# Two-layer transformer block with modulation: the modulation products in half chunks and full chunks, one bias added on TensorE

## Chip, cores, metric

One core of one Trainium2 chip runs the whole program. The metric is the device time of one execution in microseconds, as the median of several runs.

## What is computed

The program computes a first block of two layers on 256 tokens of width 1024, all in float32, and a second block on its result. Only the parts that the change touches are shown; the first layer's attention and the modulation of the second block are:

```python
# first block, layer 0: differential attention, 8 heads, 256 tokens in 2 blocks of 128 queries
sc = einsum('bqhcd,bkhcd->bhcqk', q_blk, k) * scale      # c: two score maps per head, d = 64
sc = where(causal_mask, sc + bias, NEG_INF)              # bias: T5 table by distance and head
a = softmax(sc); wts = a[:, :, 0] - lam * a[:, :, 1]
o = einsum('bhqk,bkhv->bqhv', wts, v)
mix = rms_norm(o, sub_gain) * (1 - lam_init) @ w_o
h = h + mix
h = h + conv_gated_ffn(rms_norm(h, g), w_in, conv_w, conv_b, w_out)   # width 2816, gate, conv of 3 tokens
h = h + per_layer_embedding(...)                                       # then layer 1 (latent attention), the same
# second block, for i in 0, 1: c and c_ctx are two vectors of 1024, w_mod[i] is 1024 x 3072
mod_x = silu(c) @ w_mod[i] + b_mod[i]
mod_c = silu(c_ctx) @ w_mod[i] + b_mod[i]
sh, sc, g = split(mod, 3)
hx = rms_norm(x) * (1 + sc_x) + sh_x ; ... ; x = x + g_x * yx
```

The modulation of both layers depends on nothing of the first block. It is a product of two vectors with 1024 x 6144 weights, 24 MB of float32.

## The kernel before

Every engine has an order of work written out by hand, with semaphores between them. SP loads 295 weight panels of 512 KB in turn into a ring of six (`RAW`); ACT writes the high part of each (`WH`, L1848), DVE the low part (`WL`, L1131), and PE multiplies high by high, low by high and high by low (L417 to L419) in `gemm_unit` and its kin. These are fp32r products. Plain float32 products, transposes among them, are two records each in the trace.

**Modulation.** The 24 MB are 48 panels of 128 x 1024 (512 KB), loaded by POOL's DMAs into the tile `M`. Two stages use them while PE does other work.

- The first 16 panels (`PLAIN`) are used in the first attention, `l0`. Panel `i` holds 128 output columns, with 8 groups of 128 rows. `fill(n)` (L548, called L765 to L773) issues `n` products of `SC[:, k, :]` (silu of the vectors, 128 x 32) with a 128-column tile of the panel (L558), 32 rows by 128 columns of output, float32, into the bank `O` (in the trace, `R`). There are 128 such products: 12 ahead of the attention, 5 in each of its steps up to the 18th, 14 after it, and 6 behind each of two groups of transposes. POOL loads panels in `panels` (L2494, DMA L2499), a few ahead of each `head_squares` (L2523). The squares wait for a head's output (`at_g`).
- The other 32 panels are used in the two feed-forwards, one after each of 16 tiles of a feed-forward. POOL loads them in `gathers` (L2501); ACT writes a high part (`high`, L2081), DVE a low part (`rest`, L1524), and `refill` (L571) issues four fp32r products 32 x 512 (L578) with `SCR`, the vectors in high and low part. ACT copies each finished row out (`row`, L2086 and L2139). In the embedding part (`ple`) 16 transposes of 32 x 32 (`turn_gathered`, L587) bring them to columns, and DVE sums and adds `b_mod` (`gathered`, L1420).

**Attention `l0`.** `attention` on PE (L625) takes 16 units, for each head a unit of one tile of keys (`qt` = 0) and one of two (`qt` = 1). In step n PE does the scores of unit n (`scores_l0`, L742: two maps in two row groups of 64), the filler, the value products of unit n-3 if that ended a head (`value_l0`, L750), and the transposes of unit n-2 (L651), which subtract the two maps. DVE adds the bias to the scores (`bias_l0`, L1359, 128 x 256 or 128 x 512), takes the maximum (L1212) and scales (L1187 to L1193). ACT copies the transposed weights of unit n-2 (L1887), takes the exponentials of unit n (L1898), and copies a head's output (L1997). After it come the norm over heads (POOL L2523, DVE L1364, ACT L2007, DVE L1371 and L1375), eight transposes at a time (`heads_turn`, L759), their high and low parts (ACT L2013, DVE L1384), and the projection `l0_o`.

Of the kernel before, what the change touches and what calls it, by code (L numbers as in the profile page):

```python
# [23 lines left out]
P = 128  # L24
# [5 lines left out]
PT = 8  # L30
# [7 lines left out]
MODS = 48  # L38
PLAIN = 16
GROUPS = 4  # L40
# [95 lines left out]
def program(nc, x_tok, wst, wmod, vec, cst, x_t, ctx_t, p_t, pos, pos4, tab, rpb, lam4, grow, y_t):  # L136
    with ExitStack() as ctx:
# [31 lines left out]
        SCR = sb("SCR", [P, KD, 32], F32R)  # L169
# [51 lines left out]
        RM = mv[:, 6144:12288].rearrange("p (s c) -> p s c", s=RMS)  # L221
# [43 lines left out]
        YR = B[0:32, 2048:4608]  # L265
        RR = RM[:, 0:4, :]
        RH = XH[:, 12:16, :].rearrange("p n t -> p (n t)")
        RL = XL[:, 12:16, :].rearrange("p n t -> p (n t)")
        ROWS = HRS[:, 1, 0:32].rearrange("p (r t) -> p r t", r=2)
# [61 lines left out]
        r_raw = [sem(f"r_raw{i}") for i in range(4)]  # L331
        r_hi, r_lo, r_y = sem("r_hi"), sem("r_lo"), sem("r_y")
# [76 lines left out]
        def _(pe):  # L409
# [137 lines left out]

            def fill(n):  # L548

                for _ in range(n):  # L550
                    i, k = divmod(fills[0], KD)
                    if fills[0] == 0:
# [4 lines left out]
                    out = O  # L557
                    m = mm(out[32 * g:32 * g + 32, q * P:(q + 1) * P], SC[:, k, :], RM[:, i % RMS, k * P:(k + 1) * P],  # L558
                           start=(k == 0), stop=(k == KD - 1), skip_group_check=True)
                    if k == KD - 1:  # L560
                        m.then_inc(m_used, 1)
                    fills[0] += 1

            def turn_modulators(dst):

                pe.wait_ge(m_y, 1)
                for q in range(4):
                    m = nc.tensor.transpose(dst[:, q * P:(q + 1) * P], YS[:, q * P:(q + 1) * P], IDT)
                m.then_inc(m_tr, 1)

            def refill(layer, s, i):  # L571

                if s == 0:
                    pe.wait_ge(r_y, i + (2 + 5 * layer))
                pe.wait_ge(r_lo, i * 4 + (5 + PLAIN * layer + s))
                for c in range(2):
                    for w in (RH, RL):
                        m = mm(O[0:32, :], SCR[:, 2 * s + c, :], w[:, 512 * c:512 * c + 512],  # L578
                               start=(s == 0 and c == 0 and w is RH), stop=(s == 3 and c == 1 and w is RL),
                               skip_group_check=True)  # L580
                m.then_inc(m_used, 1)

            def turn_gathered(layer):

                pe.wait_ge(r_y, 1 + 5 * (layer + 1))
                for t in range(PLAIN):
                    m = nc.tensor.transpose(O[:, 32 * t:32 * t + 32], YR[:, 512 + t * P:512 + (t + 1) * P], IDT[0:32, 0:32])  # L587
                m.then_inc(m_tr, 1)
# [36 lines left out]
            def attention(s, scores, value, filler=0, behind=None, meanwhile=(0, 0), first=0, last=None, ready=()):  # L625
                units = attn_units(s)
                width = 1 if s == "l0" else 2
                for n in range(first, len(units) + 3 if last is None else last):
# [7 lines left out]
                    if n < len(units) + 2:  # L636
                        fill(filler)
# [138 lines left out]
            turn_modulators(A[0])  # L776

            def ffn(layer):
# [37 lines left out]
                def tile(j, i=0, filled=None):  # L816
# [4 lines left out]
                    if filled is not None:  # L821
                        refill(layer, filled, i)

                if layer == 0:
                    pe.wait_ge(m_ok, 1)
                for j in range(2, 7):
# [4 lines left out]
                for d in range(3):  # L831
                    tile(19 + d)
                    refill(layer, d, 3)
                down(0, p0 + 64, hb + FT - 1, p0 + 64, False, False)
                refill(layer, 3, 3)
                down(1, p0 + 65, hb + FT, p0 + 65, False, True)

            def ple(layer):
# [7 lines left out]
                for u in range(4):  # L846
# [4 lines left out]
                    if u == 0:  # L851
                        row_parts(b, False)
                        turn_gathered(layer)
# [56 lines left out]
            attention("l1", scores_l1, value_l1, 0, first_o, (4, 3), first=2, ready=((1, TVALS),))  # L910
# [115 lines left out]
            attention("a", scores_a, value_a, 0, first_o, (2, 2), first=4)  # L1026
# [73 lines left out]
            attention("b", scores_b, value_b, 0, first_o, (6, 3), first=2, ready=((0, TVALS + 10), (1, TVALS + 12)))  # L1100
# [17 lines left out]
        def _(dv):  # L1118
# [237 lines left out]
            def bias_l0(sc, un):  # L1356
                h, qt, nk, *_ = un
                k0 = 0 if qt == 0 else P
                return v.tensor_tensor(sc, sc, bc(TB[:, h, k0:k0 + nk * P], 2), ALU.add)  # L1359
# [37 lines left out]
            def with_bias(layer, r, t0, rows):  # L1397

                n = rows.shape[-1] if len(rows.shape) == 2 else rows.shape[-1] * rows.shape[-2]
                at = VC[f"bm{layer}"] + t0  # L1400
                dst, bias = MD[:, layer, r, t0:t0 + n], V[:, at:at + n]
                if len(rows.shape) == 3:
                    dst, bias = (x.rearrange("p (g q) -> p g q", q=4) for x in (dst, bias))
# [7 lines left out]
            def modulators():  # L1411

                dv.wait_ge(m_tr, 1)
                rows = A[0].rearrange("p (q g r) -> p r g q", q=4, g=4)
                for r in range(2):
                    with_bias(0, r, 0, rows[:, r, :, :])
                scales(0)
                v.memset(SM[:, 35:36], 0.0).then_inc(m_ok, 1)

            def gathered(e, parts):  # L1420

                dv.wait_ge(m_tr, e + 1)
                link(v.tensor_reduce(ROWS, O.rearrange("p (t x) -> p t x", x=32)[:, :, 0:4].rearrange("p t (s r) -> p r t s", s=2),
                                     AX, ALU.add))
                for layer, t0, a, b in parts:
                    for r in range(2):
                        with_bias(layer, r, t0, ROWS[:, r, a:b])
                if e == 2:
                    scales(1)
                v.memset(SM[:, 35 + e:36 + e], 0.0).then_inc(m_ok, 1)  # L1430
# [20 lines left out]
            modulators()  # L1451
            dv.wait_ge(m_sil, 1)
            link(v.tensor_copy(SCR[:, :, :], SC[:, :, :]))
            link(v.tensor_tensor(SCR[:, :, 2:4], SC[:, :, 0:2], SCR[:, :, 0:2].bitcast(F32), ALU.subtract))
            v.memset(SM[:, 34:35], 0.0).then_inc(r_y, 1)
            v.memset(SM[:, 39:40], 0.0).then_inc(r_lo, 4)
# [20 lines left out]
            def ffn(layer):  # L1477
# [43 lines left out]
                def rest(s, i):  # L1521

# [1213 lines left out]
```

## Time and profile before

| | |
|---|---|
| median of 3 runs | 1325.74 us |
| lowest, highest | 1325.57, 1326.34 us |
| profiled execution, span from first to last instruction | 1325.0 us (its own time is not listed apart from the span) |
| mean granted TensorE clock | 0.998 |
| busy: PE, DVE, ACT, POOL | 1271.4, 945.7, 723.9, 391.0 us |
| attention `l0` with its end | about 98.8 to 149.3 us of the span |
| feed-forward of layer 0, of layer 1: most of each | 155 to 390, 640 to 805 us |

Matmul records overlap, so their lengths add up to more than the time they take; the time from one start to the next is what PE pays. The chain of waits gives its pieces that way. A view by lines gives busy time, the mean length of one record, and the idle time before it with what ended it.

### The profile page before, as it was taken

The numbers are of one execution on the slowest core, as the hardware profiler recorded it, in microseconds if no ns is written. First come the engines' busy times: TensorE is split into PE (matmuls) and PEld (weight loads), VectorE is DVE, ScalarE is ACT, GpSimd is POOL, SyncE is SP. The second block draws the span as 40 slices with busy tenths as digits, with TensorE's granted clock in tenths as the row PEclk, the third lists the DMA queues.
The fourth block names the chain that finished last, engine by engine and source line by source line (L and its number), as shares of the span: only waits on it lengthen the run. The fifth ranks groups of instructions, "written<-read, shape, count | busy, mean of one in ns | idle before, by whom it ended". The sixth has DMA issues, their size and how long they took to land.

```text
span 1325.0 us, 24391 instructions
## 1 busy us (share of the span) xinstructions
PE 1271.4 (96%) x8908; PEld 1102.8 (83%) x8908; DVE 945.7 (71%) x1426; ACT 723.9 (55%) x1257; POOL 391.0 (30%) x377
## 2 busy tenths in 40 slices
PE   5999999999999999999999999999989999999996
PEld 4887899999999877898999998888855699987666
DVE  6878588888878985558988887853377548454674
ACT  5555455655567777545565657644366515413562
POOL 4942144545431140143445452011012320000022
PEclk9999999999999999999999999999999999999999
DMA  8565246666645542155576663322200274522100
GB/s 309 178 218 191 72 141 233 219 222 219 217 154 172 160 130 96 63 191 171 197 234 211 230 213 128 130 93 95 96 1 1 59 181 133 170 95 80 48 1 32
DMA packets 52665, 191.72 MB, mean 145 GB/s; under 512 B 6048, under 2 KB 6304, under 8 KB 52320
## 3 DMA queue, kind: packets, MB, share of 16 engines
q1 hardware_dynamic: 43488, 158.59, 36.2%
q0 software_dynamic: 8368, 31.33, 7.5%
q8 instruction: 62, 1.02, 0.3%
q10 hardware_dynamic: 720, 0.57, 0.2%
q14 instruction: 27, 0.22, 0.0%
HBM read 189.41 MB, written 1.05 MB: 144 GB/s over the span
## 4 chain that ended last, share of the span: by engine, by line
PE 78%; DVE 9%; ACT 7%; issue 3%; POOL 1%; DMA 1%; SPq 0%; DVEq 0%; ACTq 0%; POOLq 0%
PE G L417 13%; PE G L419 13%; PE G L418 13%; PE A L417 6%; PE A L419 6%; PE A L418 6%; DVE WL L1131 3%; PE R L651 3%; PE R L578 2%; PE R L558 2%; ACT WH L1848 2%; PE A L999 1%; PE R L417 1%; PE R L419 1%; PE R L418 1%
## 5 line engine op out<-in xcount | busy, mean ns | idle before, releaser
L1131 DVE TENSOR_TENSOR WL<-RAW,WH 128x1024 fp32r<-128x1024 f32 x295 | 390.4, 1330 | 245.3 <-ACT WH L1848 244.9
L1848 ACT ACTIVATE WH<-RAW 128x1024 fp32r<-128x1024 f32 x295 | 310.4, 1057 | 387.1 <-PE G L419 275.9
L417 PE MATMUL G<-XH,WH 128*128 128x256 f32 (+1 forms) x1336 | 398.7, 298 | 7.8 <-DVE WL L1131 4.6
L419 PE MATMUL G<-XH,WL 128*128 128x256 f32 (+1 forms) x1336 | 395.4, 296 | 0.0
L418 PE MATMUL G<-XL,WH 128*128 128x256 f32 (+1 forms) x1336 | 395.4, 296 | 0.0
L417 PEld LDWEIGHTS G<-XH,WH 128*128 128x128 f32 x1336 | 255.5, 191 | 21.6 <-issue 10.6
L418 PEld LDWEIGHTS G<-XL,WH 128*128 128x128 f32 x1336 | 255.6, 191 | 7.4
L419 PEld LDWEIGHTS G<-XH,WL 128*128 128x128 f32 x1336 | 255.7, 191 | 6.2
L417 PE MATMUL A<-HH,WH 128*128 128x256 f32 x352 | 99.9, 284 | 1.0 <-POOL HL L2477 1.0
L418 PE MATMUL A<-HL,WH 128*128 128x256 f32 x352 | 99.8, 283 | 0.0
L419 PE MATMUL A<-HH,WL 128*128 128x256 f32 x352 | 99.7, 283 | 0.0
L2453 POOL CAST XH<-HRS 128x256 fp32r<-128x256 f32 x24 | 11.4, 474 | 267.3 <-DVE HRS L1745 267.3
L1212 DVE TENSOR_REDUCE SM<-A 128x2 f32<-128x1024 f32 (+1 forms) x80 | 67.7, 849 | 17.9 <-PE A L999 12.8
L417 PEld LDWEIGHTS A<-HH,WH 128*128 128x128 f32 x352 | 67.6, 192 | 2.2 <-ACT WH L1848 1.9
L1887 ACT ACTIVATE ATT<-R 128x1024 f32<-128x1024 f32 (+3 forms) x56 | 37.7, 674 | 56.8 <-PE R L651 56.8
L418 PEld LDWEIGHTS A<-HL,WH 128*128 128x128 f32 x352 | 67.6, 192 | 0.1
L419 PEld LDWEIGHTS A<-HH,WL 128*128 128x128 f32 x352 | 67.6, 192 | 0.0
L417 PE MATMUL G<-WH,XH 128*128 128x512 f32 (+1 forms) x136 | 54.6, 402 | 12.8 <-DVE XL L1157 11.1
L2473 POOL TENSOR_TENSOR HRS<-ATT,HRS 128x256 f32<-128x256 f32 x22 | 32.0, 1452 | 110.3 <-ACT HRS L2058 104.7
L2473 POOL TENSOR_TENSOR HRS<-HSQ,HRS 128x256 f32<-128x256 f32 x22 | 31.7, 1439 | 98.0 <-ACT HRS L2058 98.0
L417 PE MATMUL A<-WH,XH 128*128 128x512 f32 x144 | 57.4, 398 | 1.5 <-DVE XL L1469 1.3
L419 PE MATMUL A<-WH,XL 128*128 128x512 f32 x144 | 56.2, 390 | 0.0
(355 smaller groups left out, 2532.0 us busy)
## 6 DMA issues: line engine op xcount, KB each, us to landing
RAW<-in_wst SPq DMA_DIRECT2D x295, 512.0 KB, 4.1
M<-in_wmod POOLq DMA_DIRECT2D x48, 512.0 KB, 4.1
B<-in_rpb POOLq DMA_DIRECT2D x4, 1024.0 KB, 12.6
H<-in_x_t SPq DMA_DIRECT2D x2, 512.0 KB, 8.4
M<-in_x_tok SPq DMA_DIRECT2D x1, 1024.0 KB, 13.5
M<-in_ctx_t POOLq DMA_DIRECT2D x1, 1024.0 KB, 5.2
out_y<-M SPq DMA_DIRECT2D x2, 384.0 KB, 2.7
C<-in_cst SPq DMA_DIRECT2D x1, 737.0 KB, 15.1
```

The lines of the kernel that those rows point to most:

```text
L417: mm(out, lh, rh, start=start, stop=False, skip_group_check=True)
L418: mm(out, lh, rl, start=False, stop=False, skip_group_check=True)
L419: return mm(out, ll, rh, start=False, stop=stop, skip_group_check=True)
L558: m = mm(out[32 * g:32 * g + 32, q * P:(q + 1) * P], SC[:, k, :], RM[:, i % RMS, k * P:(k + 1) * P], start=(k == 0), stop=(k == KD - 1), s ...
L578: m = mm(O[0:32, :], SCR[:, 2 * s + c, :], w[:, 512 * c:512 * c + 512], start=(s == 0 and c == 0 and w is RH), stop=(s == 3 and c == 1 and ...
L651: m = nc.tensor.transpose(ST[c][:, k * P:(k + 1) * P], PRB[a % 3][:, c, k * P:(k + 1) * P], IDT)
L999: m = mm(out[c][:, 0:nk * P], Q2[64 * c:64 * c + 64, t, qt * P:(qt + 1) * P], K2[64 * c:64 * c + 64, t // 4, k0:512], start=True, stop=Tru ...
L1131: v.tensor_tensor(WL[:, slot, :], RAW[:, raw, :], WH[:, slot, :].bitcast(F32), ALU.subtract).then_inc(w_lo, 1)
L1212: v.tensor_reduce(small(80, a, 2), sc, AX, ALU.max, negate=True).then_inc(at_mx, 1)
L1848: act(WH[:, slot, :], RAW[:, raw, :], ACT.Copy).then_inc(w_hi, 1)
L1887: act(att(s, j)[:, 0:width, 0:nk, q * P:(q + 1) * P], RO[:, :].rearrange("p (l k q) -> p l k q", l=2, k=4)[:, 0:width, 0:nk, :], ACT.Copy) ...
L2473: g.tensor_tensor(HID[b], CB[b][:, 0, :], SG[b], ALU.mult).then_inc(f_hid, 1)
```

## The change

It has four parts.

1. **Half chunks in `l0`.** The first 2048 columns are now 8 chunks of 128 rows x 2048 columns (1 MB), each loaded as two half chunks of 512 KB. `fill(1)` multiplies one half chunk: two products 32 x 512 (L560 of the changed kernel), in float32, for two column groups of 32, each with another 512 columns. 16 such fills are made: two ahead of the attention, one in each of steps 1 to 14, none behind it.
2. **Bias on TensorE.** For the units with `qt` = 1, `scores_l0` issues two more products (L728), identity times the bias table `TB` (128 x 256, float32), which add onto the scores in PSUM. DVE adds the bias for `qt` = 0 only.
3. **Full chunks in the feed-forwards.** Eight chunks of 1 MB in each, one after tiles 6, 8, 10, ... 20. `modulate` (L547) issues four float32 products 32 x 512 in the four column groups. High and low parts, `rest`, `high`, `row` and the sums of `gathered` go; POOL copies the vectors into `SV` (128 x 32) beside each load. In `ple` four transposes of 128 x 128 take the place of the sixteen.
4. **POOL's order in `l0`.** Panels up to `8 + 2 * h` are loaded ahead of the squares of head `h`, where it was `6 + (10 * h + 35) // 8`.

```diff
+            def modulate(vectors, buf, start, stop):
+                for g in range(4):
+                    m = mm(O[32 * g:32 * g + 32, :], vectors, RM[:, buf, g, :], start=start, stop=stop, skip_group_check=True)
+                m.then_inc(m_used, 1)
...
             def fill(n):
                 for _ in range(n):
-                    i, k = divmod(fills[0], KD)
...
-                    if k == 0:
-                        pe.wait_ge(m_raw[i % RMS], 16 * (i // RMS + 1))
-                    g, q = i // 4, i % 4
-                    m = mm(out[32 * g:32 * g + 32, q * P:(q + 1) * P], SC[:, k, :], RM[:, i % RMS, k * P:(k + 1) * P],
-                           start=(k == 0), stop=(k == KD - 1), skip_group_check=True)
+                    i = fills[0]
+                    k, half = divmod(i, 2)
...
+                    pe.wait_ge(m_raw[i % RMS], 16 * (i // RMS + 1))
+                    for g in range(2):
+                        r = 32 * (2 * half + g)
+                        m = mm(O[r:r + 32, :], SC[:, k, :], RN[:, i % RMS, 512 * g:512 * g + 512],
+                               start=(k == 0), stop=(k == CHUNKS - 1), skip_group_check=True)
+                    m.then_inc(m_used, 1)
                     fills[0] += 1
...
             def attention(...):
-                    if n < len(units) + 2:
-                        fill(filler)
+                    if n in filler:
+                        fill(1)
...
             def scores_l0(out, unit):
-                           KT0[64 * c:64 * c + 64, h, 0:nk * P], start=True, stop=True, skip_group_check=True)
+                           KT0[64 * c:64 * c + 64, h, 0:nk * P], start=True, stop=qt == 0, skip_group_check=True)
+                if qt:
+                    for c in range(2):
+                        m = mm(out[c][:, 0:nk * P], IDT, TB[:, h, P:P + nk * P], start=False, stop=True, skip_group_check=True)
...
-            fill(12)
+            fill(2)
             pe.wait_ge(bias_ok, 1)
-            attention("l0", scores_l0, value_l0, 5)
-            fill(14)
+            attention("l0", scores_l0, value_l0, range(1, 15))
             heads_turn(0)
-            fill(6)
             heads_turn(1)
-            fill(6)
...
             def ffn(layer):
+                def modulated(buf, turn, start=False, stop=False):
+                    pe.wait_ge(r_vec[buf], turn + (v0 + 1))
+                    pe.wait_ge(r_raw[buf], turn * 16 + 16 * (v0 + 1))
+                    modulate(SV[:, buf, :], buf, start, stop)
                 for j in range(2, 7):
                     tile(j)
+                modulated(0, 0, start=True)
                 with pe.Fori(0, 3) as i:
-                    for d in range(4):
-                        tile(7 + d, i, d)
...
+                    tile(7, i)
+                    tile(8, i)
+                    modulated(1, i)
+                    tile(9, i)
+                    tile(10, i)
+                    modulated(0, i + 1)
...
             def bias_l0(sc, un):
-                return v.tensor_tensor(sc, sc, bc(TB[:, h, k0:k0 + nk * P], 2), ALU.add)
+                return None if qt else v.tensor_tensor(sc, sc, bc(TB[:, h, 0:P], 2), ALU.add)
...
-                upto = min(PLAIN, 6 + (10 * h + 35) // 8)
+                upto = min(PLAIN, 8 + 2 * h)
                 panels(nextp, upto)
                 nextp = upto
                 head_squares(h)
```

PE in the attention before, from the fillers of one step to the transposes of the next but one (`R` is the bank of fillers and transposes, `M` holds panels, keys and values, `m_raw0` counts landed panels of the first slot):

```order
L558 MATMUL R<-M,SC 32x128 x5
L750 MATMUL G<-M,ATT 128x128 [waits at_tc]
L750 MATMUL G<-M,ATT 128x128 x2
L651 MATMUL R<-C,RSQ 128x128 [waits at_tc,at_p]
L742 MATMUL A<-M 128x256 [waits at_ex]
L742 MATMUL A<-M 128x256
L558 MATMUL R<-M,SC 32x128
L558 MATMUL R<-M,SC 32x128 [waits m_raw0]
L558 MATMUL R<-M,SC 32x128 x3
L651 MATMUL R<-C,HSQ 128x128 [waits at_tc,at_p]
```

And PE in the attention after the change, about the same place:

```order
L735 MATMUL G<-M,ATT 128x128 [waits at_g,at_tc]
L735 MATMUL G<-M,ATT 128x128 x2
L633 MATMUL R<-C,HSQ 128x128 [waits at_tc,at_p]
L724 MATMUL A<-M 128x256 [waits at_ex]
L724 MATMUL A<-M 128x256
L728 MATMUL A<-B,C 128x256 x2
L560 MATMUL R<-M,SC 32x512 [waits m_raw0]
L560 MATMUL R<-M,SC 32x512
L633 MATMUL R<-C,ATP 128x128 [waits at_tc,at_p]
L633 MATMUL R<-C,ATP 128x128
L724 MATMUL A<-M 128x128 [waits at_ex]
L724 MATMUL A<-M 128x128
```

Five records of 128 columns have become two of 512, a wait for a landed half chunk stands ahead of each, and two products onto the scores (L728) follow the scores of every second unit.

PE in a feed-forward before, after each of 16 tiles:

```order
L575 REGISTER_ALU [waits r_y]
L578 MATMUL R<-XH,SCR 32x512 [waits r_lo]
L578 MATMUL R<-XL,SCR 32x512
L578 MATMUL R<-XH,SCR 32x512
L578 MATMUL R<-XL,SCR 32x512
```

And after the change, after every second tile:

```order
L413 MATMUL A<-HH,WH 128x256
L414 MATMUL A<-HL,WH 128x256
L415 MATMUL A<-HH,WL 128x256
L547 MATMUL R<-M,SV 32x512 [waits r_raw0,r_vec0]
L547 MATMUL R<-M,SV 32x512 x3
```

Four fp32r products with one wait for DVE's low part have become four float32 products with waits for POOL's copy and for the load.

POOL in the attention before, between the first squares and the last:

```order
L2499 DMA M<-in_wmod 128x1024 [waits m_used] x4
L2523 TENSOR_TENSOR HRS<-B 128x2x128 [waits at_g]
L2499 DMA M<-in_wmod 128x1024 [waits m_used]
L2523 TENSOR_TENSOR HRS<-B 128x2x128 [waits at_g]
L2499 DMA M<-in_wmod 128x1024 [waits m_used]
L2523 TENSOR_TENSOR HRS<-B 128x2x128 [waits at_g]
L2499 DMA M<-in_wmod 128x1024 [waits m_used] x2
L2523 TENSOR_TENSOR HRS<-B 128x2x128 [waits at_g]
L2499 DMA M<-in_wmod 128x1024 [waits m_used]
```

POOL after the change, the rows that answer to these:

```order
L2452 DMA M<-in_wmod 128x1024 [waits m_used] x2
L2478 TENSOR_TENSOR HRS<-B 128x2x128 [waits at_g]
L2452 DMA M<-in_wmod 128x1024 [waits m_used] x2
L2478 TENSOR_TENSOR HRS<-B 128x2x128 [waits at_g]
L2452 DMA M<-in_wmod 128x1024 [waits m_used] x2
L2478 TENSOR_TENSOR HRS<-B 128x2x128 [waits at_g]
L2452 DMA M<-in_wmod 128x1024 [waits m_used] x2
L2478 TENSOR_TENSOR HRS<-B 128x2x128 [waits at_g]
L2452 DMA M<-in_wmod 128x1024 [waits m_used] x2
```

Where one load or two stood between the squares of two heads, there are now two each time: panels 8 and 9 behind the squares of head 0, used by steps 7 and 8, and so on up to panels 14 and 15 behind those of head 3, used by steps 13 and 14.

## Rows read from the trace of the kernel before

**Rows 1.** The page: span, busy time of the engines.
```profile
span 1325.0 us, 24391 instructions
...
PE 1271.4 (96%) x8908; PEld 1102.8 (83%) x8908; DVE 945.7 (71%) x1426; ACT 723.9 (55%) x1257; POOL 391.0 (30%) x377
```

**Rows 2.** Windows: span, busy us of PE, PEld, DVE, ACT, POOL; clock; DMA share.
```profile
98.80:133.00 34.20, 34.20 (x270) 25.75 (x269) 29.50 (x72) 17.04 (x75) 8.28 (x15) 1.00 0.53 186
133.00:149.30 16.30, 14.67 (x119) 11.90 (x115) 11.24 (x20) 8.03 (x23) 3.70 (x5) 1.00 0.09 33
235.00:390.00 155.00, 154.13 (x1227) 146.99 (x1227) 132.35 (x151) 90.62 (x123) 70.18 (x61) 1.00 0.64 210
```

**Rows 3.** Chain of waits, 238 to 252: start us, us, what.
```profile
240.52 0.92 PE R L578 x4
```

**Rows 4.** Waits of PE, 235 to 390: what ended them, us, times, longest.
```profile
PE R L578 <- DVE XL L1524: 0.4, 1, 0.4
```

**Rows 5.** Chain, 96 to 150: attention's start, one pair of units, its end.
```profile
96.09 2.78 PE R L558 x24
...
113.88 0.63 PE A L742 x4
...
115.73 0.37 PE R L651 x2
...
116.52 1.21 PE R L558 x10
...
118.70 0.63 PE A L742 x4
...
139.47 0.94 PE G L750 x6
...
145.53 0.20 ACT SM L2007
...
147.99 1.43 PE R L558 x12
```

**Rows 6.** Chain, 960 to 975: products in row groups and in column groups.
```profile
962.16 1.06 PE A L999 x4
963.22 1.04 PE R L651 x8
...
966.79 1.13 PE A L999 x4
...
970.77 1.88 PE G L1008 x16
```

**Rows 7.** Line 485: min/median/max ns, first and last start, forms.
```profile
L485 PE MATMUL R<-RSQ,C x8: 376/379/380, 394.3 to 395.8; 128*128 128x256 f32 x8
```

**Rows 8.** Lines by form, 96 to 133: busy us, mean ns, idle before.
```profile
L1359 DVE TENSOR_TENSOR A<-A,B 128x512 f32<-128x512 f32 x7 | 4.9, 698 | 2.3 <-PE A L742 2.3
...
L1898 ACT ACTIVATE RSQ<-A,SM 128x256 f32<-128x256 f32 x6 | 2.8, 470 | 1.6 <-DVE SM L1212 1.6
L2523 POOL TENSOR_TENSOR HRS<-B 128x256 f32<-128x256 f32 x4 | 2.4, 606 | 16.1 <-ACT B L1997 16.1
L1887 ACT ACTIVATE ATT<-R 128x256 f32<-128x256 f32 x6 | 2.3, 383 | 7.4 <-PE R L651 7.4
...
L1997 ACT ACTIVATE B<-G 128x256 f32<-128x256 f32 x5 | 1.9, 390 | 0.0
```

**Rows 9.** Issues, 96 to 145: xcount, KB each, median us to landing.
```profile
M<-in_wmod POOLq DMA_DIRECT2D x12, 512.0 KB, 4.8
RAW<-in_wst SPq DMA_DIRECT2D x1, 512.0 KB, 3.7
```

**Rows 10.** Lines by form, 133 to 149.4.
```profile
L1364 DVE TENSOR_REDUCE SM<-HRS 128x8 f32<-128x1024 f32 x2 | 2.4, 1217 | 0.5 <-POOL HRS L2523 0.5
```

**Rows 11.** Line 587: min/median/max ns, first and last start, forms.
```profile
L587 PE MATMUL R<-C,B x16: 220/222/243, 396.1 to 397.1; 32*128 32x32 f32 x16
```

**Rows 12.** Lines of DVE, 235 to 390.
```profile
L1524 DVE TENSOR_TENSOR XL<-M,XH 128x1024 fp32r<-128x1024 f32 x16 | 27.6, 1723 | 0.0
```

More of the change, by code:

```diff
@@ L330, in program @@
         sum_step = sem("sum_step")
-        r_raw = [sem(f"r_raw{i}") for i in range(4)]
-        r_hi, r_lo, r_y = sem("r_hi"), sem("r_lo"), sem("r_y")
+        r_raw = [sem(f"r_raw{i}") for i in range(2)]
+        r_vec = [sem(f"r_vec{i}") for i in range(2)]
         h_sq = sem("h_sq")
@@ L583, in turn_gathered @@
[L583 to L587, printed above, removed]
                 m.then_inc(m_tr, 1)
@@ L623, in advance, with attention @@
                     next(unit, None)
-            def attention(s, scores, value, filler=0, behind=None, meanwhile=(0, 0), first=0, last=None, ready=()):
+            def attention(s, scores, value, filler=(), behind=None, meanwhile=(0, 0), first=0, last=None, ready=()):
                 units = attn_units(s)
@@ L909, in _ @@
                                 + [(1, k) for k in range(8, 16)], T, lambda k: pe.wait_ge(at_g, AJ0["l1"] + k // 2 + 1))
-            attention("l1", scores_l1, value_l1, 0, first_o, (4, 3), first=2, ready=((1, TVALS),))
+            attention("l1", scores_l1, value_l1, (), first_o, (4, 3), first=2, ready=((1, TVALS),))
             advance(first_o, 32)
@@ L1025, in _ @@
             evacuated(pe, U0["a_z"] + 7)
-            attention("a", scores_a, value_a, 0, first_o, (2, 2), first=4)
+            attention("a", scores_a, value_a, (), first_o, (2, 2), first=4)
             advance(first_o, KD)
@@ L1397, in with_bias @@
             def with_bias(layer, r, t0, rows):
-                n = rows.shape[-1] if len(rows.shape) == 2 else rows.shape[-1] * rows.shape[-2]
+                n = rows.shape[-1] * rows.shape[-2]
                 at = VC[f"bm{layer}"] + t0
-                dst, bias = MD[:, layer, r, t0:t0 + n], V[:, at:at + n]
-                if len(rows.shape) == 3:
-                    dst, bias = (x.rearrange("p (g q) -> p g q", q=4) for x in (dst, bias))
+                dst, bias = (x.rearrange("p (g q) -> p g q", q=4) for x in (MD[:, layer, r, t0:t0 + n], V[:, at:at + n]))
                 link(v.tensor_tensor(dst, rows, bias, ALU.add))
@@ L1409, in scales, with modulators @@
                                             bc(V[:, VC[f"ng{layer}"]:VC[f"ng{layer}"] + 8], 2), ALU.add, ALU.mult))
[L1411 to L1424, printed above, removed]
+            def modulators(made, src, parts):
+                dv.wait_ge(m_tr, made)
+                rows = src.rearrange("p (q g r) -> p r g q", q=4, g=4)
                 for layer, t0, a, b in parts:
                     for r in range(2):
[L1427 to L1430, printed above, removed]
+                        with_bias(layer, r, t0, rows[:, r, a:b, :])
+                if made != 2:
+                    scales(made // 2)
+                v.memset(SM[:, 34 + made:35 + made], 0.0).then_inc(m_ok, 1)
             def add_out(tag, per, gain, late):
@@ L2075, in lands @@
                     return [16 * ((p + 3 + d) // RAWS + 1) for d in range(3)]
-                def high(s, i):
-                    ac.wait_ge(r_raw[s], i * 16 + (64 * layer + 16))
-                    ac.wait_ge(m_used, i * 4 + (PLAIN * (layer + 1) + s))
-                    act(RH, RR[:, s, :], ACT.Copy).then_inc(r_hi, 1)
-                def row(i, used):
-                    ac.wait_ge(m_used, used)
-                    act(YR[:, bass.ds(i * 512, 512)], O[0:32, :], ACT.Copy).then_inc(r_y, 1)
                 for j in range(2, 6):
```

101 lines of the change are left out of this document (34 added, 67 removed).

## The prediction

> **What bounds the kernel now.** I first read the page: the span is 1325.0 us and PE is busy for 96% of it [rows 1]. Then I read the windows of the three places that the change touches. In the attention PE has no idle time at all (34.20 of 34.20 us), and in a feed-forward nearly none (154.13 of 155.00). Only the end of the attention has 1.6 us [rows 2]. So what counts is what PE pays for each product, from start to start, and I read that in the chain of waits, since the records overlap. Work taken from DVE or ACT is worth nothing by itself under a PE that never waits; it counts only in the end of the attention, where the chain runs over several engines. The executions are 1325.57 to 1326.34 us, and the span is 0.74 us below their median; I add the sum of the changes to the median, 1325.74. What differs by less than 0.2%, 2.65 us, I call the same.
>
> **Feed-forwards.** Removed: 32 groups of four products (L578), each 0.92 us of PE [rows 3], so 29.4 us. Added: 16 chunks of four float32 products of 512 columns in the four column groups. One such product alone is two records. L485 shows eight records of 256 columns starting within 1.5 us, that is 0.214 each [rows 7]; a record of 512 costs 0.43 and a product 0.86. What do four in different column groups cost? The trace has only pairs. Two products 64 x 512 in two row groups take 1.06 us [rows 6], against 1.72 one behind the other, and the 0.2 above one product is the price of going in and out of that form. Sixteen records of 256 columns in two column groups (L1008) take 1.88 us where 16 x 0.214 = 3.4 would be due [rows 6], so column groups pair as well. If four groups go side by side as two do, a chunk costs 0.86 + 0.2, which I round up to C = 1.1. If only two go at once it is 2 x 0.86 + 0.2 = 1.9, and if none do it is 3.6. The lower end is 0.86. I take 1.1, since both kinds of groups show the full gain of their number. That gives 16 x 1.1 = 17.6 us, and the feed-forwards gain 29.4 - 17.6 = **11.8 us**. The change breaks even here at C = 1.84.
>
> The Trainium skill, "TensorE: Matmul & The Clock Gate", Part 3 (Packing small matmuls), has three column tiles of 32 with 512 columns as 2.38 times faster, and four row tiles as 3.07 times. An estimate by the latter is 4 x 0.86 / 3.07 = 1.12 us a chunk, about my value; no row here shows four tiles.
>
> DVE's `rest` (16 in the window, 1.7 us each) goes too [rows 12]. PE waits for it once in the window, 0.4 us [rows 4]; two such waits, one for each feed-forward, are **-0.8**. ACT's `high` and `row` hide behind PE and count nothing. The new waits of a chunk are for POOL's copy and its 1 MB, issued behind the gate product of the tile two before; some 1.5 tiles, over 12 us, lie between, against 4.8 us for half the size [rows 9], 9.6 if twice as long. I price them at nothing. Behind POOL's wait for a used buffer stands the gate work of the next tile; that buffer was used a tile earlier, so it does not wait either.
>
> In the embedding parts sixteen transposes, first to last start 1.0 us and so about 1.1 in all [rows 11], become four that at two records of 128 columns take 0.43: 2 x 0.67 is **-1.3**.
>
> **Attention, PE's work.** A pair of units now takes 118.70 - 113.88 = 4.82 us, with two fillers of 1.21 [rows 5]. Each becomes a pair of products of 512 columns in two column groups, 1.06 by the pair in row groups [rows 6], so -0.3 for a pair of units. The bias of the second unit is two full products of 256 columns, 4 x 0.214 = 0.86 [rows 7], and 0.1 for one more change of form: +0.95. The pair becomes 5.45. Over the attention that is 8 x 0.95 = 7.6, less 14 x 0.15 = 2.1, less the fillers of the steps that have none now. Of those four, two (steps 0 and 15) are on PE's path and two lie in the drain, where PE waits for the chain through DVE anyway: 7.6 - 2.1 - 1.8 = **+3.7 us**, with the last of them taken at half. The 2.78 us of filler ahead [rows 5] is nearly all cover: the start waits for `bias_ok` at 98.7. DVE loses eight additions of 0.70 [rows 8], but it follows PE there and gives nothing back.
>
> **Attention, the panels.** This is the part to look at. The fill of step 7 needs panel 8, which POOL issues only behind the squares of head 0. Those need ACT's copy of head 0's output in step 5. From then on one fill hangs on the other in a ring: fill 1.06, transposes 0.37 [rows 5], then ACT's copy of weights 0.38, two exponentials 0.94 and the copy out 0.39, POOL's squares 0.61 [rows 8], the issue, and the landing of 512 KB. The landing is 3.7 us in an emptier stretch of the same window and 4.8 as the median of the present panels, which go out in bursts [rows 9]. The ring closes in 3.75 + 3.7 = 7.45 to 3.75 + 4.8 = 8.55 us, for two steps that otherwise take 5.45. The loads will be two at a time with little beside them, so I take the short end, 2.0 us for each of the fills of steps 7, 9, 11 and 13: **+8.0 us**, with 12.4 as the upper end and 0 as the lower one (if the squares ran earlier than I read). Queued behind the waiting fill on PE are the transposes and the scores of the next unit, so all of it is lost.
>
> The skill's "DMA: Bandwidth & Descriptors" (Anatomy of one DMA) gives 2.0 us plus bytes over 436,000, an estimate of 3.2 us; by it the ring would be 6.95 and this term +6.0. The rows with 3.7 and more decide.
>
> **End of the attention.** Between the last value product at 139.47 and the projection now lie 28 + 12 filler products. Those ahead of `heads_turn` keep ACT's high parts late, and the root (L2007, 145.53) stands behind them in ACT's queue [rows 5]. Without them the root waits for DVE's sum alone, which ends at 143.25 (1.22 us [rows 10]): about 2.0 earlier. The last six products, 1.43 us at 147.99 [rows 5], go as well. Of these 3.4 us I keep **-2.9**, because the low parts that the first products of the projection need are now late next.
>
> **Sum.** 3.7 + 8.0 - 2.9 - 11.8 - 1.3 - 0.8 = -5.1, so 1320.6 us; I say **1320.5**.
>
> **Rivals.**
> - *Only two column groups go at once* (the slower side). Each chunk costs 1.9, and 16 x 0.8 = 12.8 us are added to the forecast: 1333.4 us, about 1333.5. It decides from C = 1.42 on, where the sum of all parts is above nothing (5.1 / 16 more than 1.1). For it: no stretch of the trace has more than two groups at work, and the four products have four different moving operands of 512 float32 columns. Against it: the pairs lose nothing. 0.17.
> - *The ring does not close.* If POOL's loads come a step earlier than I read, the 8.0 us is not there: 1312.6 us. Against it is the order of POOL, where the load stands behind the squares of the head before. 0.14.
> - *The products after a stall are dear, or the stalls are longer than 2.0.* PE will stand still four times in the attention, and landings of 4.8 give 4.4 us more: 1325 us. The granted clock is 1.00 in all windows, and two products behind a pause of PE from 964.26 to 966.79 took 1.13 against 1.06 [rows 6], so a pause of that size does not cost speed. A longer thin stretch is not in the trace. 0.14.
>   A rule of the skill's "TensorEngine Tiling (Array Packing)", Key Properties, speaks against the change too: a change of tiling mode drains TensorE. The trace agrees with some 0.2 us for a change in and out [rows 6], and this is in the terms.
> - *All four in turn*, C = 3.6: 40 us more, 1360. Nothing but a lack of evidence speaks for it: 0.02.
>
> The forecast itself has 0.53. **How the numbers follow.** The forecast's own spread, from a C of 0.9 to 1.25 and a landing that is 0.3 shorter to 0.6 longer, is 1317 to 1325. It is faster by over 0.2% (below 1323.1) in some four of five cases. With the second rival the chance of faster is 0.44 + 0.14 = 0.58. The same (1323.1 to 1328.4) gets 0.09 of the forecast and half of the third rival: 0.16. Slower has the first and the last rival and the rest of the third: 0.26. The range must take in the second and the first rival: 1311 to 1334.
>
> **What would show each step.** A start of the next product 1.1 us after the first of four in the feed-forwards; waits of PE's filler on a load in steps 7, 9, 11 and 13 of about 2 us; pairs of units of 5.45 us before them; some 7 us from the last value product to the projection. A chunk near 2 us, or a filler that finds its panel always there, would make the prediction wrong.

## The result and the profile after

The changed kernel takes 1335.78 us as the median of four runs (1331.67 to 1337.36), beside 1326.04 for the kernel before in the same series. The ratio is 1.0067, with a 95% interval of 1.0049 to 1.0084: slower, where 1320.5 was forecast, and just above the range of 1311 to 1334. A second series gave 1335.2 and a ratio of 1.0065 (1.0051 to 1.0078). One execution of `e6_ffn_last` below took 1960.5 us at a mean clock of 0.586, a slow state of the chip, and its ratio leaves it out.

From the page of the changed kernel, the lines that answer to [rows 1], and the granted clock in 40 slices of 33 us:

```profile
span 1332.6 us, 23842 instructions
...
PE 1264.5 (95%) x8724; PEld 1077.7 (81%) x8724; DVE 878.7 (66%) x1380; ACT 689.6 (52%) x1217; POOL 365.5 (27%) x377
...
PEclk9998799999999999999999999999999999999999
```

PE has less to do (1264.5 us of busy records for 1271.4) and the span is 7.6 us longer. (The profiled execution took 1334.25 us, one of the two shorter ones; between the medians lie 9.7 us, and the profile can account for 7.6 of them.) The clock row has a dent in the fourth and fifth slice, 100 to 167 us. The windows of that stretch (us, busy us of PE, PEld, DVE, ACT, POOL, then granted clock, DMA share, GB/s) show when it falls:

```profile
96.00:150.00 54.00, 45.23 (x203) 20.34 (x203) 26.41 (x70) 17.05 (x75) 9.09 (x16) 0.84 0.39 135
116.00:118.00 2.00, 0.34 (x2) 0.00 (x0) 1.46 (x4) 0.00 (x0) 0.00 (x0) 1.00 0.82 283
118.00:120.00 2.00, 1.35 (x4) 0.19 (x4) 0.00 (x0) 0.00 (x0) 0.00 (x0) 0.56 0.57 234
...
134.00:136.00 2.00, 0.57 (x2) 0.19 (x4) 0.59 (x2) 0.00 (x0) 0.00 (x0) 0.82 0.85 340
136.00:138.00 2.00, 2.00 (x8) 0.38 (x4) 0.00 (x0) 0.00 (x0) 0.00 (x0) 0.50 0.02 6
156.00:166.00 10.00, 7.49 (x31) 6.17 (x31) 7.06 (x11) 4.65 (x10) 1.22 (x2) 0.50 0.00 0
166.00:176.00 10.00, 10.00 (x85) 10.00 (x85) 3.90 (x5) 3.98 (x5) 1.04 (x1) 1.00 0.30 92
```

Of the attention's 54 us PE is busy for 45 and not for 52 as before, and the mean clock is 0.84. Each fall to 0.5 (1.2 GHz) follows a stretch in which PE was nearly idle: 0.34 us busy in 116 to 118, then a mean of 0.56; 0.57 us in 134 to 136, then 0.50. From the end of the drain (the last steps, in which PE waits for the chain through DVE) the clock stays at 0.5 for ten whole microseconds, into the projection. Here is the chain of waits of the attention (start us, us, what): its start, one turn of the ring, the starts of the next two, and its end:

```profile
97.58 1.54 PE A L724 x8
99.13 2.00 PE A L728 x4
...
118.65 1.92 PE R L560 x4
120.57 0.63 PE R L633 x2
...
121.51 1.01 ACT RSQ L1866 x4
122.52 0.28 ACT B L1965
...
122.88 0.56 POOL HRS L2478
123.44 4.08 DMA M<-in_wmod
...
127.56 1.05 PE R L560 x4
128.61 0.39 PE R L633 x2
...
135.43 1.92 PE R L560 x4
...
144.38 1.05 PE R L560 x4
...
156.98 1.65 PE G L735 x6
```

From the fill at 118.65 the chain goes over the transposes, ACT's exponentials and copy of a head's output (122.52), POOL's squares (122.88) and a load (123.44 to 127.52) to the next fill at 127.56. That is the ring that the prediction describes, and it turns in 8.91 us, then 7.87, then 8.95. The first and the third turn begin at half clock: the fill costs 1.92 and not 1.05, the transposes 0.63 and not 0.39. In the list of waits the filler has (total, times, longest):

```profile
PE R L560 <- DMA M<-in_wmod: 7.2, 4, 2.4
```

A feed-forward, the chain at two chunks, and the waits of PE in most of it:

```profile
247.66 1.00 PE R L547 x8
...
266.12 1.00 PE R L547 x8
```

```profile
PE A L413 <- POOL HL L2431: 1.9, 1, 1.9
```

The eight records of a chunk take 1.00 us. Two tiles and a chunk take 18.46 us (266.12 - 247.66). Before, the panel behind the one at 240.52 [rows 3] was this:

```profile
250.06 0.92 PE R L578 x4
```

So a tile with its panel took 250.06 - 240.52 = 9.54 us, and two of them 19.08. A tile alone is 72 products that start 0.12 us apart, 8.64 us. With that a chunk costs 1.18 us in all (the 1.00, 0.09 on the way in and 0.10 on the way out), and a panel of before 0.90.

Where the 7.6 us of the span come from, by the starts of the same product in both traces: at the first product of the projection `l0_o` the changed kernel is 15.1 us behind (164.47 against 149.35), at its end 15.8. The first feed-forward gives back 4.2, the embedding part nothing, the second feed-forward 4.1. The profiled kernels also reach their first scores at different times, 97.4 to 99.6 us. Two programs that are the same up to the end of the attention (`e4_ffn_only` and `e6_ffn_last` below) do so at 98.34 and 99.57, so a difference of 1 to 2 us there says nothing of an edit. Where two attentions are compared below, it is from the first scores on.

### The profile page after: what moved, and what is told of

The parts are those of the page before. It is cut to its first block, busy times and chain, and to the rows that moved or that the text cites. A ratio compares the mean times of both kernels' runs of the same rounds, so it can differ in the third digit from the quotient of the medians.

```text
span 1332.6 us, 23842 instructions
## 1 busy us (share of the span) xinstructions
PE 1264.5 (95%) x8724; PEld 1077.7 (81%) x8724; DVE 878.7 (66%) x1380; ACT 689.6 (52%) x1217; POOL 365.5 (27%) x377
## 3 DMA queue, kind: packets, MB, share of 16 engines
HBM read 189.41 MB, written 1.05 MB: 143 GB/s over the span
## 4 chain that ended last, share of the span: by engine, by line
PE 77%; DVE 8%; ACT 7%; issue 3%; DMA 2%; POOL 1%; SPq 0%; DVEq 0%; ACTq 0%; POOLq 0%
PE G L413 14%; PE G L415 13%; PE G L414 13%; PE A L413 6%; PE A L415 6%; PE A L414 6%; PE R L633 3%; DVE WL L1123 3%; ACT WH L1816 2%; PE R L413 1%; PE R L415 1%; PE R L414 1%; PE A L991 1%; DMA M<-in_wmod 1%; PE G L1000 1%
## 5 line engine op out<-in xcount | busy, mean ns | idle before, releaser
L1123 DVE TENSOR_TENSOR WL<-RAW,WH 128x1024 fp32r<-128x1024 f32 x295 | 382.5, 1304 | 289.8 <-ACT WH L1816 289.4
L414 PE MATMUL A<-HL,WH 128*128 128x256 f32 x352 | 99.6, 283 | 0.0
```

Source lines behind the costliest of these rows:

```text
L414: mm(out, lh, rl, start=False, stop=False, skip_group_check=True)
L1123: v.tensor_tensor(WL[:, slot, :], RAW[:, raw, :], WH[:, slot, :].bitcast(F32), ALU.subtract).then_inc(w_lo, 1)
```

## Experiments

Each kernel ran in five rounds beside the kernel before, 4 to 11 executions of each. Medians are compared with the median of before in the same series. What is read from a trace stands for one execution.

**The late loads alone.** Is the ring what makes the attention long, or would the clock fall without it?

```diff
-                upto = min(PLAIN, 8 + 2 * h)
+                upto = min(PLAIN, 10 + 2 * h)
```

> The changed kernel, with POOL's loads in the first attention issued two panels earlier (up to 10 + 2h ahead of the squares of head h), so that no fill waits for a load that stands behind the squares of the head before. Ring theory (each of the fills of steps 7, 9, 11 and 13 waits for squares and landing, and the half clock in that stretch comes from these pauses): the four periods of 7.9 to 8.9 us fall to about 5.5, granted clock 1.00 up to the drain, 12 to 14 us less than the changed kernel, about 1320. Rival (the ring costs its waits, but the clock falls because PE has 16 us less work in the attention, ring or not): about 8 us less, about 1328, and the clock stays near 0.85 in that stretch.

It took 1322.19 us (before 1326.62; ratio 0.9973, 0.9963 to 0.9983): some 13 us less than the changed kernel, by one number in POOL's order, and this version is faster than before. The chain has one load at its start, issued behind the flag `bias_ok`, for which PE does not stand still. Behind it come plain pairs of units and no further load:

```profile
99.77 6.11 DMA M<-in_wmod
...
115.78 1.06 PE A L728 x4
116.84 0.98 PE R L560 x4
...
121.20 1.06 PE A L728 x4
```

A pair takes 121.20 - 115.78 = 5.42 us, forecast 5.45. The bias costs 1.06 (L728), the half chunk 0.98 (L560). The end still falls to half clock:

```profile
139.00:142.00 3.00, 1.26 (x7) 0.88 (x7) 2.89 (x7) 2.86 (x8) 0.63 (x2) 1.00 0.00 0
142.00:152.00 10.00, 6.55 (x26) 5.23 (x27) 6.91 (x12) 4.15 (x11) 1.83 (x3) 0.55 0.00 0
```

From the fill of step 5 to the bias products of step 15, the stretch that holds the four waiting fills, the trace has 26.05 us here (111.42 to 137.47) and 39.42 in the changed kernel (110.92 to 150.34): 13.4 less. So the ring theory holds for size; the rival is right about the drain, which is at half clock with or without the ring.

**The late loads kept, the bias back on DVE.**

```diff
-                if qt:
-                    for c in range(2):
-                        m = mm(out[c][:, 0:nk * P], IDT, TB[:, h, P:P + nk * P], start=False, stop=True, skip_group_check=True)
...
-                return None if qt else v.tensor_tensor(sc, sc, bc(TB[:, h, 0:P], 2), ALU.add)
+                k0 = 0 if qt == 0 else P
+                return v.tensor_tensor(sc, sc, bc(TB[:, h, k0:k0 + nk * P], 2), ALU.add)
```

> The changed kernel with the bias back on DVE, the late loads kept. Ring theory: the ring has no bias product in it, so its four periods stay at 7.9 to 8.9 us and only the pairs outside it get shorter, 3 to 4 us less than the changed kernel, about 1332. Rival (the bias products are what makes the attention long, and the waits for panels only fill the room): 8 us less, about 1327.

1335.02 us (1326.62; 1.0057, 1.0044 to 1.0071), the same as the changed kernel within their spread: the 3 to 4 us that I gave it can't be seen in the total. (The trace has 64.9 us from the first scores to the projection for 66.9, so up to 2 us may be there.) Most of the PE work that is gone comes back as waiting, 13.1 us for loads where it was 7.2:

```profile
PE R L560 <- DMA M<-in_wmod: 13.1, 5, 3.7
```

**Both.** Loads early and bias on DVE:

> As e1_early, and the bias of the two-tile units back on DVE (the eight pairs of identity products are gone). If PE sets the attention's pace without the ring, each of eight units gives back 1.0 us: 7 to 8 us under e1_early, about 1313. If the chain through DVE and ACT sets it, DVE gets 0.7 us more for each and nothing is gained: the same as e1_early, within 2 us.

1316.6 us (1326.62; 0.9932, 0.9918 to 0.9945), 5.6 us under the early loads alone, where 7 to 8 were expected. PE sets the pace once the ring is open. The eight pairs of bias products are worth 8.5 us of PE, but at the start PE now comes earlier to the fill of step 3, whose load POOL issues behind `bias_ok`, and waits for it; with the bias on PE it did not.

```profile
PE R L560 <- DMA M<-in_wmod: 2.1, 1, 2.1
```

```profile
97.83 6.54 DMA M<-in_wmod
104.41 1.05 PE R L560 x4
...
108.84 0.98 PE R L560 x4
...
113.20 0.98 PE R L560 x4
```

Its pairs take 113.20 - 108.84 = 4.36 us.

**The bias alone**, in the kernel before: the same two products after the scores and DVE's addition for `qt` = 0 only, nothing else.

> The kernel before, with nothing but the bias of the two-tile units moved to TensorE. PE has no idle time in that attention, so each of eight units pays two full products, 1.06 us by the trace of the changed kernel: pairs of 5.9 us where they took 4.82, 8 us slower than before, about 1334.5, clock 1.00. Rival (DVE's 0.7 us less for each unit shortens a chain that PE waits for): 3 us slower or less.

1334.9 us (1326.49; 1.0059, 1.0045 to 1.0073), 8.4 us slower. In the chain:

```profile
111.31 0.63 PE A L742 x4
111.94 1.06 PE A L746 x4
...
117.19 0.63 PE A L742 x4
```

A pair takes 117.19 - 111.31 = 5.88 us, 1.06 more than before, at full clock. Eight of them are 8.5.

**The feed-forwards alone.** Attention, its fillers, POOL's order and the layout of the first 16 panels as before; feed-forwards and embedding parts as changed.

```diff
-                    for g in range(2):
-                        r = 32 * (2 * half + g)
-                        m = mm(O[r:r + 32, :], SC[:, k, :], RN[:, i % RMS, 512 * g:512 * g + 512],
...
+                    m = mm(O[32 * g:32 * g + 32, q * P:(q + 1) * P], SC[:, k, :], RN[:, i % RMS, k * P:(k + 1) * P],
...
                     if n in filler:
-                        fill(1)
+                        fill(5)
...
-            fill(2)
+            fill(12)
             pe.wait_ge(bias_ok, 1)
-            attention("l0", scores_l0, value_l0, range(1, 15))
+            attention("l0", scores_l0, value_l0, range(18))
+            fill(14)
             heads_turn(0)
+            fill(6)
             heads_turn(1)
+            fill(6)
...
-                upto = min(PLAIN, 8 + 2 * h)
+                upto = min(PLAIN, 6 + (10 * h + 35) // 8)
```

> The change in the feed-forwards alone: the attention has the fillers, the loads, the layout of its panels and the bias on DVE of before. By the two traces the feed-forwards give 4.1 to 4.2 us each: 8.3 us under before, 1317.5 to 1318.5. Rival (the gain there is tied to loads or to a semaphore that the attention's end sets): under 5 us, above 1321.

1318.4 us (1326.62; 0.9941, 0.9928 to 0.9955): 8.2 us less. The attention's 15.8 us less these 8.2 give the 7.6 of the span.

**Cover for the end of a feed-forward.** The 1.9 us wait for POOL above stands at the last down product, where before had a panel.

```diff
-                modulated(1, 3, stop=True)
                 tile(21)
                 down(0, p0 + 64, hb + FT - 1, p0 + 64, False, False)
+                modulated(1, 3, stop=True)
                 down(1, p0 + 65, hb + FT, p0 + 65, False, True)
```

> The change in the feed-forwards alone, with the last chunk of each multiplied between the last two down products, where the last panel of before stood, and not after tile 20. If the 1.9 us that PE waits there for POOL's low part is what before covered with its last panel, the chunk covers 1.1 us of it in each feed-forward: 2 us under the feed-forward change alone (e4_ffn_only), 3.5 us if the half clock behind that wait in the first feed-forward goes too, 1315 to 1316.5. Rival (the end is set by the embedding part behind it, which waits for the modulation rows now later): no change, 1318.

1315.66 us (1326.49; 0.9916, 0.9901 to 0.9932), 2.7 us under the feed-forwards alone. The waits in the first feed-forward, of the kernel without the cover and then with it:

```profile
PE A L413 <- POOL HL L2432: 1.8, 1, 1.8
```

```profile
PE A L413 <- POOL HL L2432: 0.9, 1, 0.9
```

and the clock behind the wait, in the same order:

```profile
376.00:382.00 6.00, 6.00 (x40) 6.00 (x39) 2.29 (x5) 2.11 (x4) 0.00 (x0) 0.72 0.29 95
```

```profile
376.00:382.00 6.00, 6.00 (x52) 6.00 (x52) 3.79 (x7) 3.52 (x8) 0.00 (x0) 1.00 0.27 93
```

In this execution some 3.4 us at half clock follow the wait of 1.8 us (a mean of 0.72 over six), and none follow the one of 0.9. Of the nine changed programs whose trace has a wait of 1.8 to 1.9 us there, four have such a fall and five have none, the changed kernel among these. So the shorter wait is sure, and what the cover gives by the clock isn't shown by these two traces alone.

**Fills two steps later.** Loads early, bias on DVE, and `range(3, 17)` for the steps that fill.

> As e2_early_dve, with the fills in steps 3 to 16 and not 1 to 14. In e2_early_dve the fill of step 3 waits for a load that POOL issues behind the bias flag (landing 6.5 us later), and the drain has no filler and falls to half clock. Now that load is used in step 5 and the drain has two fillers. Expected by the theory of pauses: the wait of step 3 goes (2 to 3 us) and some of the half clock in the drain (0 to 2 us), 1312 to 1314.5. Rival (the two fills in the drain lie on the chain through DVE and give it all back): 1316 to 1317.

1317.22 us (1326.49; 0.9931, 0.9917 to 0.9944): no gain, a miss for me. The wait for the load is gone, but the first steps have no filler now, and the window 100 to 105 us is at 0.50, 105 to 110 at 0.74, where the loads early with the bias on DVE had 1.00 in both. From the first scores to the projection it takes 47.3 us for 46.9: what the wait had cost, the clock took.

**All of it**: early loads, bias on DVE, later fills, and the cover at the ends of the feed-forwards.

> e7_later_fills and the last chunk of each feed-forward as cover of the last wait (as e6_ffn_last). If the two gains are apart they add: e7_later_fills less what e6_ffn_last is under e4_ffn_only, about 1311. If not, as e7_later_fills.

1313.8 us (1326.49; 0.9905, 0.989 to 0.992). The cover's 2.7 us add to the rest (3.4 here); it is not 1311, because the step before it gave nothing.

**More work, to hold the clock.** How much is the clock's own share? Products with a stationary operand of zeros add nothing to the rows but keep PE busy. In the changed kernel, loads late:

```diff
+            def cover(n):
+                for _ in range(n):
+                    mm(O[0:32, 0:P], SV[:, 0, :], IDT, start=False, stop=False, skip_group_check=True)
...
+                    if s == "l0" and n in (7, 9, 11, 13):
+                        cover(10)
                     if n in filler:
                         fill(1)
```

> The changed kernel with more work for PE: ten products with a stationary operand of zeros (they add nothing to the rows) ahead of each of the four fills that wait for a load, 2.4 us of work inside each wait of some 2 to 3 us; the loads stay late. If the half clock comes from PE's pauses, all four periods are now 7.9 us and none is 8.9, and the steps behind them run at full clock: 2 to 4 us less than the changed kernel, about 1332 to 1333. Rival (the clock falls for another reason, or the ring is set by full pauses alone): no gain, 1335 to 1337.

1334.07 us (1325.76; 1.0052, 1.0038 to 1.0066). Up to the drain the attention is at full clock now. The turns of the ring take 8.05 us (118.36 to 126.41), 7.79, and 8.51 behind a load of 4.67:

```profile
126.00:129.00 3.00, 2.75 (x16) 0.79 (x14) 0.67 (x2) 1.13 (x5) 0.00 (x0) 1.00 0.33 132
...
150.00:157.00 7.00, 4.06 (x17) 3.22 (x16) 4.50 (x8) 3.68 (x9) 2.45 (x4) 0.65 0.00 0
```

```profile
118.36 1.05 PE R L560 x4
...
126.41 1.05 PE R L560 x4
...
134.20 1.01 PE R L560 x4
...
142.71 1.05 PE R L560 x4
```

From the fill of step 5 to the bias products of step 15 it takes 36.6 us (110.58 to 147.14) where the changed kernel took 39.4: the clock's share in the ring is some 2.9 us. The projection starts 3.2 us earlier than in the changed kernel, but 1.0 us of what was gained lies ahead of all cover: the first scores ran at full clock in this execution. The total shows less of it, since this execution has half clock behind the waits at the ends of the feed-forwards; with intervals that overlap, the total alone would not decide. So I ran the changed kernel again beside a kernel with cover in the drain as well:

> The changed kernel itself, once more, beside e12_ring_drain_cover on the same chip: 1333 to 1338, granted clock 0.986 to 0.991, the longer times at the lower clocks.

> As e9_ring_cover, and five products of zeros in each of steps 14 to 18 and six ahead of each group of the last transposes as well, with the last fill put between these. If PE's pauses bring the half clock, the attention and its end run at 1.00, the ring still costs its waits (four periods of about 8), and it is 5 to 6 us less than the changed kernel, about 1330. Rival (added work stands on the chain of the drain): no less than e9_ring_cover, 1333 to 1335.

1335.2 and 1333.56 us (1326.75; 1.0065, and 1.0053 with 1.0039 to 1.0066). From 104 us to the end of the attention the clock is whole, in 150 to 165 us too, where the changed kernel run again had 0.70 (150 to 166):

```profile
104.00:150.00 46.00, 44.22 (x272) 25.67 (x269) 22.69 (x59) 16.04 (x70) 7.33 (x12) 1.00 0.35 120
```

But 1.6 us is all it gives, not 5 to 6, and the intervals overlap. The ring still closes at full clock in 7.85 us (127.62 to 135.47), once in 9.4 behind a load of 5.5 us. The products of zeros in the drain stand on the chain: from the bias products of step 15 to the projection it takes 15.1 us at full clock (149.52 to 164.59), where the changed kernel took 14.1 with the last ten at half. Both sides of my expectation are half right: filling the pauses holds the clock, and holding it with idle work costs most of what it gives.

**The best version with cover**: the version above (early loads, bias on DVE, covered ends) with products of zeros ahead of the bias flag, in steps 0 to 2 and 15 to 18 and ahead of the last transposes.

> e8_all with such products of zeros where its PE stands still and its clock is half: 8 ahead of the bias flag, 5 in each of steps 0 to 2 and 15 to 18, 6 ahead of each group of the last transposes; the last two fills one and two places later. If the pauses cause the half clock, granted clock is 1.00 all through the attention, and it is 2 to 4 us less than e8_all, about 1310 to 1312, with more work on PE. Rival (the added products stand on the chain): the same or 1 to 3 us more.

1312.24 us (1325.76; 0.9900, 0.9886 to 0.9914), clock 1.00 in all of the attention, and PE busy for 53 of its 54 us:

```profile
96.00:150.00 54.00, 53.00 (x361) 32.81 (x360) 42.60 (x98) 26.67 (x98) 11.33 (x20) 1.00 0.40 133
```

It and the version without zeros (0.9905) can't be told apart by their intervals. From the first scores to the projection it is even a little longer, 47.1 us for 46.6. Both are faster than before and than the changed kernel.

## Why the prediction was wrong, point by point

- **Which mechanism.** The prediction called the panels the part to look at, and the ring is there, at the four steps that it names, in the order of links that it gives. Its size was off: the term of +8.0 us measured 13.4 in the traces, and some 13 in the medians (1335.8 against 1322.2). "The ring closes in 3.75 + 3.7 = 7.45" was the smaller part of that. At full clock it is 7.87, the links 3.86 and the landing 4.01; four times 7.87 less the pair's 5.42 is 9.8. The 3.7 us for the landing were a panel of SP's queue; POOL's own panels, where they went out singly in the trace before, took 3.8 to 4.2. The other 3.6 us are mostly the half clock, since two turns of three and the step behind the last begin with it; the cover in the ring gave 2.9 of them back.
- **The clock.** "A pause of that size does not cost speed" was the step that failed most, and with it the chance of 0.14 for the rival that named it. The reading under it was wrong. From 964.26 to 966.79 the chain of waits runs over other engines, but PE was not standing still; it worked there, and its two waits were 0.57 and 0.71 us:

```profile
965.45 0.63 PE L651 MATMUL R<-C,ATP 128*128 128x128 f32 x4 [0.57 <-ACT ATT L1887]
966.79 1.13 PE L999 MATMUL A<-M 64*128 64x512 f32 x4 [0.71 <-ACT RSQ L1898]
```

  So the trace before held no pause of PE of the ring's size behind the first 25 us, and nothing to price one by. The change made six of 1.7 to 2.5 us between 96 and 166 us, and some 27 us at 1.2 GHz: about 3 at the start, 14 in the ring and 10 at the end. The longer executions also have the lower mean clock (1331.7, 1334.3, 1337.3 and 1337.4 us with 0.991, 0.987, 0.986 and 0.986), which fits; that the clock makes all of that spread isn't shown.
- **The pair of units.** 5.42 us measured, 5.45 forecast; the half chunk 0.98 for 1.06, the bias 1.06 for 0.95. With the ring closed the bias costs nothing that the total shows (late loads, bias on either engine: the same time); alone it costs 8.4. Terms that were added in the sum are really a maximum: a ring closed by a load, or PE's own work.
- **The end of the attention.** From the last value product to the projection 7.5 us (156.98 to 164.47), forecast 7.0 against 9.9 before: right in kind, and half a microsecond short. The last eight transposes take 1.97 us at half clock where they took 1.26, which would be enough for it; no run settles this, since the kernels with full clock there have added work on the chain. The start came 1.2 us earlier than before (97.58 against 98.82), but that lies within what same programs differ by.
- **The feed-forwards.** C = 1.18 us, forecast 1.1; the rival with two column groups at a time (1.9) falls. The removed panels cost 0.90 rather than 0.92. 32 x 0.90 - 16 x 1.18 = 9.9 where the prediction had 11.8. The waits of a chunk, priced at nothing, are nothing, and the -0.8 for DVE's `rest` came. What failed here is that all removed panels were counted as gain: the one behind the second-last down product was itself cover. Without it PE waits 1.9 us for POOL and not 0.5, in each feed-forward. 9.9 + 0.8 - 2 x 1.4 = 7.9, and the traces give 8.3, the kernel with the feed-forwards alone 8.2. The forecast was 11.8 + 0.8 = 12.6.
- **The embedding parts.** -1.3 forecast, nothing found. The chain through that stretch runs over ACT, POOL and DVE and has no transposes in it, in either kernel. Here it is in the changed one, where PE has four transposes to do and the kernel before had sixteen:

```profile
404.21 1.07 ACT B L2065 x2
...
405.79 1.28 ACT L1840
...
409.41 1.76 DVE RST L1138
```

  I priced PE's records without asking the chain whether PE was on the path there.
- **In one sum.** The span grew by 7.6 us, where 5.1 less was forecast. Of the difference of 12.7 us, 7.0 are in the attention and the projection (15.8 for 8.8), 4.3 in the feed-forwards (8.3 for 12.6), and 1.3 in the embedding parts. The 15.8 are, by the traces: an earlier start, -1.2; half clock behind the start, 1.5; PE's own work, 3.9 (read from the version with early loads; forecast 3.7); the ring, 13.4 (forecast 8.0); the end, -2.4 (forecast -2.9); half clock in the projection, 0.7 (the parts are rounded). So PE's own work was right, and nearly all that was missing is the ring and the clock.

## What to carry to other kernels

When a load is issued behind work that itself waits for the consumer of the load before, write the ring down and add every link at its measured length; then compare it with the work that it competes with, and take the larger, not the sum. Before a pause is priced by a row, look whether the engine itself stood still there: a gap between its pieces in the chain of waits is not yet idle time. When filler is halved, ask of each place where it stood what it covered: here a landing, a last wait for POOL, and PE's clock. And open a ring by the order of issue first: one number in POOL's order was worth more than any of the work that was saved.

## What was not expected of the hardware

- Four float32 products of 512 columns in four column groups of 32 cost 1.00 us from first to last, where one alone would cost 0.86 by the prediction's estimate from records of 256 columns [rows 7]; with the way in and out 1.18. The records of the four start 7 ns apart. The Trainium skill, "TensorE: Matmul & The Clock Gate", Part 3, has 3.07 times for four row tiles. 4 x 0.86 / 1.00 is 3.4 times here for four column groups, and 2.9 with the way in and out, so the page's 3.07 lies between the two.
- In the changed kernel the granted clock falls to 1.2 GHz after PE's waits of 2.0, 2.3, 2.4 and 2.5 us, and after one of 1.7 at the start of the attention, which it did not do in `e9_ring_cover`. A wait of 2.1 us in `e2_early_dve` (before 104.41) was not followed by a fall. In the first feed-forward a single wait of 1.8 to 1.9 us for POOL was followed by it in some traces (`e4_ffn_only`, `e9_ring_cover`) and not in others (the changed kernel, `e1_early`), and none of the waits of 0.9 us was. The Trainium skill, "TensorE: Matmul & The Clock Gate", "HAM oscillation", tells of waits for loads that bring the gated clock again and again; the windows above agree with it, at 0.5 behind the thin stretches of 116 to 118 and 134 to 136 us.
- The first of two loads of 512 KB that POOL issues in the ring takes 3.9 to 4.2 us from issue to landing, the first of four behind the bias flag 6.1 to 6.6. The Trainium skill, "DMA: Bandwidth & Descriptors" (Anatomy of one DMA), gives an estimate of 3.2; the measured landings decide.
